# Turning one tile of widened reciprocal roots instead of eight tiles of scaled x, with x also loaded as columns

## What is computed

```python
def rms_norm(x, g):
    y = x * lax.rsqrt(jnp.mean(x * x, axis=-1, keepdims=True) + RMS_EPS)
    return y * g
u = rms_norm(h, pre_norm[l])                      # 4096 x 1024
proj = jnp.einsum('bsd,de->bse', u, w_in[l])      # 4096 x 3072
```

## Time and profile before

| | |
|---|---|
| device time, median of 3 | 2173.83 us |
| profiled execution: its time, its span | 2177.77 us, 2175.6 us |
| PE busy | 2055.3 us (94%) |
| DVE busy | 1561.1 us (72%) |
| ACT busy | 1350.1 us (62%) |
| POOL busy | 115.2 us (5%) |
| moved by DMA | 401.40 MB, mean 184 GB/s |

### The profile page before, as it was taken

The page is one execution under the profiler, slowest core; times in us unless marked ns, Lnnn a source line. Parts: engine busy times, 40 slices in busy tenths (PEclk is TensorE's granted clock), DMA queues, the critical chain, the costliest instruction groups (busy, mean ns, idle before and its releaser), DMA issues. The chain is left out here.

```text
span 2175.6 us, 39344 instructions
## 1 busy us (share of the span) xinstructions
PE 2055.3 (94%) x12892; PEld 1717.4 (79%) x12892; DVE 1561.1 (72%) x4410; ACT 1350.1 (62%) x3520; POOL 115.2 (5%) x116
## 2 busy tenths in 40 slices
PE   5999799999999999998889999999899998899998
PEld 4787678888888888886777888888778887688886
DVE  6575574546655574445589899799799997888887
ACT  6453454544555464343699999899689997533333
POOL 1232210000000000001200000000000000000000
PEclk7999999999999999999899999899999999999999
DMA  4466666768577757578976686596869895355543
GB/s 156 151 218 221 179 227 174 227 206 249 159 224 233 201 191 243 197 246 259 219 146 129 128 173 135 115 179 120 164 147 214 228 267 168 103 164 174 171 158 114
DMA packets 351736, 401.40 MB, mean 184 GB/s; under 512 B 105616, under 2 KB 255248, under 8 KB 346688
## 3 DMA queue, kind: packets, MB, share of 16 engines
q1 hardware_dynamic: 343120, 364.80, 61.2%
q0 software_dynamic: 8432, 34.30, 5.2%
HBM read 255.62 MB, written 143.39 MB: 183 GB/s over the span
## 5 line engine op out<-in xcount | busy, mean ns | idle before, releaser
L854 PE MATMUL p_ps<-p_u_hi,p_w_hi 128*128 128x512 f32 x1344 | 537.3, 400 | 36.3 <-DVE p_p_c L739 17.1
L856 PE MATMUL p_ps<-p_u_hi,p_w_lo 128*128 128x512 f32 x1344 | 528.7, 393 | 0.0
L855 PE MATMUL p_ps<-p_u_lo,p_w_hi 128*128 128x512 f32 x1344 | 528.4, 393 | 0.0
L570 DVE TENSOR_TENSOR p_w_lo<-p_w_raw,p_w_hi 128x512 fp32r<-128x512 f32 x336 | 250.6, 747 | 340.2 <-ACT p_w_hi L423 338.5
L1621 ACT ACTIVATE probs<-probs,a_stat 128x256 f32<-128x256 f32 (+1 forms) x896 | 433.4, 489 | 50.3 <-DVE a_stat L1455 47.1
L423 ACT ACTIVATE p_w_hi<-p_w_raw 128x512 fp32r<-128x512 f32 x336 | 210.7, 628 | 339.1 <-PE p_ps L856 297.9
L854 PEld LDWEIGHTS p_ps<-p_u_hi,p_w_hi 128*128 128x128 f32 x1344 | 255.7, 190 | 96.3 <-issue 17.8
L856 PEld LDWEIGHTS p_ps<-p_u_hi,p_w_lo 128*128 128x128 f32 x1344 | 255.4, 190 | 55.0
L855 PEld LDWEIGHTS p_ps<-p_u_lo,p_w_hi 128*128 128x128 f32 x1344 | 256.0, 190 | 51.3
L1455 DVE CUSTOM_DVE_ANT_0 probs<-a_ps_s,fixed 128x256 f32<-128x256 f32 (+1 forms) x704 | 251.2, 396 | 56.4 <-PE a_ps_s L1354 53.1
L1408 PE MATMUL a_ps_o<-a_pT,a_v 128*64 128x128 f32 x3320 | 256.3, 285 | 23.6 <-ACT a_pT L1645 21.9
(11 more groups left out here) (202 smaller groups left out, 2752.5 us busy)
## 6 DMA issues: line engine op xcount, KB each, us to landing
p_w_raw<-in_w_in SPq DMA_DIRECT2D x156, 256.0 KB, 3.5
p_w_raw<-scratch_w_s SPq DMA_DIRECT2D x144, 256.0 KB, 3.6
scratch_qk_hi<-p_out_a SPq DMA_DIRECT2D x80, 256.0 KB, 4.0
scratch_qk_lo<-p_out_b SPq DMA_DIRECT2D x80, 256.0 KB, 3.9
a_v<-scratch_v SPq DMA_DIRECT2D x40, 512.0 KB, 7.7
scratch_gate<-p_out_a SPq DMA_DIRECT2D x64, 256.0 KB, 3.9
scratch_v<-p_out_a SPq DMA_DIRECT2D x256, 64.0 KB, 2.3
a_gate<-scratch_gate SPq DMA_DIRECT2D x64, 256.0 KB, 6.1
```

What stands on the lines that cost most here:

```text
L570: nc.vector.tensor_tensor(w_lo[:, m % 3, :, :], w_raw[:, entry(j, g), :, :], w_hi[:, m % 3, :, :].bitcast(F32), ALU.subtract).then_inc(w_l ...
L854: nc.tensor.matmul(bank, hi, u_hi[j][:, k, :], start=j < 2 and k == 0, stop=False, skip_group_check=True)
L855: nc.tensor.matmul(bank, hi, u_lo[j][:, k, :], start=False, stop=False, skip_group_check=True)
L856: last = nc.tensor.matmul(bank, lo, u_hi[j][:, k, :], start=False, stop=k == KH - 1, skip_group_check=True)
```

## The change

x is given to the kernel a second time, transposed (`x_columns`, 1024 x 4096). It is loaded straight to the place in `raw` where the turned rows were put. The rows of x are still loaded, for the squares alone. ACT's `scale` goes away. DVE spreads the 128 reciprocal roots of a tile, one per partition, over 128 columns (`widen`); PE turns this one block, so that every partition holds the roots of the 128 tokens along its row; and DVE multiplies the eight blocks of columns by them and by the gain of the channel, in place, with eight instructions instead of one.

```diff
+        spread = sb("spread", [P, P])
-        def front_bank(t):
-            place = (0, 1, 2, 0, 2, 0, 2, 0)[t]
+        def front_place(t):
+            place = (0, 1, 3, 5, 6, 0, 1, 5)[t]
+            return (ps_t[:, place, 0:P] if place < 2 else ps[:, place - 2, 0:P])
...
                 def load_x_first(t):
                     if t >= 4:
-                        sp.wait_ge(u_turned, t - 3)
+                        sp.wait_ge(squared, t - 3)
...
+                def load_columns(c, done):
+                    sp.dma_start(raw[:, c, :, :], io["x_columns"].rearrange("(k p) n -> p k n", p=P)[
+                        :, :, c * CHUNK:(c + 1) * CHUNK]).then_inc(done, 16)
...
+                load_x_first(2)
+                load_x_first(3)
+                load_columns(0, m_stored)
                 for j in (0, 3, 4, 6):
                     load_w(j, 0)
-                load_x_first(2)
-                load_x_first(3)
-                for t in range(4, XT):
-                    load_x_first(t)
+                load_x_first(4)
+                load_x_first(5)
+                sp.wait_ge(consts, 48)
+                load_columns(1, consts)
+                load_x_first(6)
+                load_x_first(7)
...
-                def scale(n, src):
-                    act.wait_ge(inverted, n + 1)
-                    nc.scalar.activation(src, src, ACT.Copy, scale=ss[:, n % 2, 3:4]).then_inc(scaled, 1)
...
+                def widen(n):
+                    dve.wait_ge(inverted, n + 1)
+                    if n:
+                        dve.wait_ge(u_turned, n)
+                    nc.vector.tensor_copy(spread[:], ss[:, n % 2, 3:4].broadcast_to([P, P])).then_inc(scaled, 1)
+
-                def keep(n, src):
+                def keep(n, roots):
                     dve.wait_ge(u_turned, n + 1)
...
-                    nc.vector.tensor_tensor(raw[:, t // 4, :, (t % 4) * P:(t % 4 + 1) * P], src.rearrange("p a (k n) -> p (a k) n", n=P),
-                                            gain[:].unsqueeze(2).broadcast_to([P, KD, P]), ALU.mult).then_inc(raw_ready, 1)
+                    if quarter and t == 0:
+                        dve.wait_ge(ahead.w_loaded, 32 * quarter)
+                    for k in range(KD):
+                        place = raw[:, t // 4, k, (t % 4) * P:(t % 4 + 1) * P]
+                        last = nc.vector.scalar_tensor_tensor(out=place, in0=roots, scalar=gain[:, k:k + 1], in1=place,
+                                                              op0=ALU.mult, op1=ALU.mult)
+                    last.then_inc(raw_ready, 1)
...
+                def turn_roots(n, dst):
+                    pe.wait_ge(scaled, n + 1)
+                    nc.tensor.transpose(dst, spread[:], ident[:]).then_inc(u_turned, 1)
...
+                def load_columns(quarter):
+                    pool.wait_ge(u_lo_ready, NJ * quarter)
+                    for c in range(2):
+                        at = quarter * QT + c * CHUNK
+                        pool.dma_start(raw[:, c, :, :], io["x_columns"].rearrange("(k p) n -> p k n", p=P)[
+                            :, :, at:at + CHUNK]).then_inc(ahead.w_loaded, 16)
...
-                        pool.wait_ge(u_turned, n)
+                        pool.wait_ge(squared, n)
...
+                    if i == 0 and g >= NP:
+                        load_columns(quarter + 1)
```

More of the change, by code:

```diff
@@ L405, in _ @@
                     slot(G, j)
-                sp.wait_ge(m_stored, 48)
+                sp.wait_ge(m_stored, 64)
                 for b in range(3):
@@ L432, in high_u @@
                     elif j == 6:
[L433 removed]
+                        act.wait_ge(squared, XT)
                     nc.scalar.activation(u_hi[j][:], u_raw[j], ACT.Copy).then_inc(u_hi_ready, 1)
@@ L483, in _ @@
                     root(t)
-                    scale(t, x_first[:, t % 4, :])
                     if t in (1, 2):
@@ L531, in slot @@
                             root(n)
-                        if j == 2:
-                            scale(n, x_next)
                     if quarter == 3 and i == 1:
@@ L584, in add_u @@
                         dve.wait_ge(raw_ready, XT * (quarter + 1))
-                        dve.wait_ge(u_turned, XT * (quarter + 1))
+                        dve.wait_ge(squared, XT * (quarter + 1))
                     else:
@@ L600, in invert @@
                     nc.vector.reciprocal(ss[:, b, 3:4], ss[:, b, 2:3]).then_inc(inverted, 1)
-                def keep(n, src):
+                def widen(n):
[4 more added lines that the diff above has]
+                def keep(n, roots):
                     dve.wait_ge(u_turned, n + 1)
+                    quarter, t = divmod(n, XT)
                     if n == 0:
                         dve.wait_ge(consts, 48)
-                    t = n % XT
-                    nc.vector.tensor_tensor(raw[:, t // 4, :, (t % 4) * P:(t % 4 + 1) * P], src.rearrange("p a (k n) -> p (a k) n", n=P),
-                                            gain[:].unsqueeze(2).broadcast_to([P, KD, P]), ALU.mult).then_inc(raw_ready, 1)
+                        dve.wait_ge(m_stored, 16)
+                    if n == 4:
+                        dve.wait_ge(consts, 64)
+                    if quarter and t == 0:
[5 more added lines that the diff above has]
+                    last.then_inc(raw_ready, 1)
                 def low(g, block):
@@ L706, in _ @@
                     invert(t)
+                    widen(t)
                     if t:
-                        keep(t - 1, front_bank(t - 1))
+                        keep(t - 1, front_place(t - 1))
                     if t in (2, 3):
@@ L712, in _ @@
                         low_u(0, FIRST[t - 6])
-                keep(XT - 1, front_bank(XT - 1))
+                keep(XT - 1, front_place(XT - 1))
                 add_u(0, "T1")
@@ L746, in differ @@
                     if n == 0:
-                        dve.wait_ge(ahead.w_loaded, 16 * KD)
-                        dve.wait_ge(m_stored, 48)
+                        dve.wait_ge(ahead.w_loaded, 96 + 16 * KD)
+                        dve.wait_ge(m_stored, 64)
                     else:
@@ L783, in slot @@
                             invert(n)
+                            widen(n)
                         if j == 4:
-                            keep(n, ps_t[:])
+                            keep(n, ps_t[:, 0, 0:P])
                     if quarter < 3 and i == NP - 2 and j in (1, 4):
@@ L827, in turn @@
                     last.then_inc(done, 1)
+                def turn_roots(n, dst):
+                    pe.wait_ge(scaled, n + 1)
+                    nc.tensor.transpose(dst, spread[:], ident[:]).then_inc(u_turned, 1)
                 for t in range(XT):
-                    pe.wait_ge(scaled, t + 1)
-                    if t >= 3:
-                        pe.wait_ge(raw_ready, (1, 3, 4, 5, 6)[t - 3])
-                    turn(t, x_first[:, t % 4, :], front_bank(t), u_turned)
+                    if t >= 5:
+                        pe.wait_ge(raw_ready, (1, 2, 4)[t - 5])
+                    turn_roots(t, front_place(t))
                 def product(g, j):
@@ L897, in slot @@
                         n = (quarter + 1) * XT + t
-                        pe.wait_ge(scaled, n + 1)
                         pe.wait_ge(raw_ready, n)
                         wait_v(g)
-                        turn(n, x_next, ps_t, u_turned)
+                        turn_roots(n, ps_t[:, 0, 0:P])
                     if quarter == 3 and i in (2, 3) and j == 3:
@@ L954, in _ @@
                     nc.gpsimd.tensor_tensor(s4, a12, s2, ALU.subtract).then_inc(w_added, 1)
+                    if g == 1:
+                        load_columns(1)
                 pool.wait_ge(multiplied, NJ * (3 * NP + 4) + 7)
@@ L1908, in _ @@
                 rounds(act, scalar_round, lambda g: g.scalar_parts(act))
-                act.wait_ge(ahead.w_loaded, 16 * KD + 48)
+                act.wait_ge(ahead.w_loaded, 96 + 16 * KD + 48)
                 act.wait_ge(groups[1].values_done, groups[1].TOTAL)
```

7 lines of the change are left out of this document (3 added, 4 removed).

## The result

| | before | changed |
|---|---|---|
| device time, median | 2175.01 us (2167.49 to 2193.32, 18 runs) | 2185.14 us (2175.91 to 2196.52, 18 runs) |
| profiled execution: time, span | 2177.77, 2175.6 us | 2180.97, 2179.2 us |
| PE, DVE, ACT busy | 2055.3, 1561.1, 1350.1 us | 2030.6, 1594.9, 1317.0 us |
| moved by DMA | 401.40 MB | 418.17 MB |

The ratio of changed to before is 1.0046, 95% interval 1.003 to 1.0063. The forecast was 2165 us, the range 2156 to 2180: the result lies outside it and on the other side of no change. In the second batch of runs (experiment 1) the same kernel came to 1.0057. PE's busy time fell by 24.7 us, and the kernel is about 10 us slower.

What follows compares the result with a forecast made beforehand. PE was taken to bound projection quarters 1 to 3, the making of first operands its start. Terms: -18.5 steady tiles, +2 first quarter, +1.5 joins, +6 front, +0.5 late rows = -8.5 us, giving a 2165 us median, range 2156 to 2180.

Steps and rivals of the forecast that it cites:

- three places to cost: The 24 steady tiles, the front with its 8 tiles, and the new loads.
- Quarter 1's have 5 us more: Columns of quarters 2 and 3 are needed only at 370.38 us; those of quarter 1 have 5 us more.
- The term I had for the first quarter: Eight of 24 turns (6.2 us) lie where PE sometimes waits for weights; 2 us given back, bounds 0 and 6.2.
- Steady tiles: PE in 24 tiles: seven of eight transposes go, 0.77 us a tile, 18.5 us gained, bounds 10.6 and 21.
- the joins: DVE's longer `keep` delays the second `join`: 0.5 us for one tile a quarter, 1.5 us lost, bounds 0 and 6.
- DVE's duration: `keep` as eight pieces of 128 columns takes 2.1 us, 0.9 more than now, bounds 1.1 and 2.7.
- overlap down to 1.1: Rival, more gain: DVE's eight pieces overlap to 1.1 us and loads don't hold the front; 2159 us, chance 0.18.
- The front: Start of the projection: late rows and four longer keeps start T1 at 41.7 instead of 35.74; 6 us lost.
- Rows behind the columns: Rows queued behind 4.2 MB of columns on POOL's queue land 3 us early; 0.5 us lost, bounds 0 and 18.
- The rival that carried my chance for slower: Rows behind the columns land 6.6 us late and cost 9 us, for quarters 2 and 3; 2183 us, chance 0.12.

Runs made afterwards that it cites:

- experiment 1: The changed kernel run again, unedited, for a second trace; 2186.88 us, ratio 1.0057 to the kernel before.
- experiment 3: The kernel before plus POOL's 4.2 MB load of quarter 1's columns, used for nothing; 2178.90 us, ratio 1.0018 to the kernel before.
- experiment 7: The changed kernel with only one of eight channel groups of quarter 1's columns loaded (0.5 MB); 2180.70 us, ratio 1.0014 to the kernel before.
- experiment 5: The changed kernel with the front (tiles 0 to 7) made the old way, burst kept; 2182.17 us, ratio 1.0034 to the kernel before.
- experiment 12: The changed kernel with the old front and an eighth of quarter 1's columns loaded; 2170.85 us, ratio 0.9977 to the kernel before.
- experiment 8: The changed kernel with `keep` as one instruction, without the gain; 2180.57 us, ratio 1.0024 to the kernel before.
- experiment 9: Only tiles 16 to 31 new, and `keep` one slot later in groups 8 and 9; 2162.49 us, ratio 0.9938 to the kernel before.
- experiment 2: The changed kernel with tiles 0 to 15 made the old way, only 16 to 31 new; 2165.11 us, ratio 0.9967 to the kernel before.
- experiment 4: The changed kernel with tiles 8 to 15 made the old way, so new front and no burst; 2178.53 us, ratio 1.0022 to the kernel before.
- experiment 6: The changed kernel with the second 2.1 MB columns load of a quarter issued three groups later; 2186.72 us, ratio 1.0058 to the kernel before.
- experiment 11: The changed kernel with the front's two columns loads cut to an eighth, POOL filling in ones; 2184.07 us, ratio 1.0035 to the kernel before.
- experiment 10: Only tiles 16 to 31 made the new way, run again unedited; 2164.82 us, ratio 0.9958 to the kernel before.

## Why the prediction was wrong

**The step that failed: the first quarter and its loads.** The prediction named three places to cost, and priced the burst of columns by one victim alone, the rows behind it on POOL's own queue, for quarters 2 and 3; of quarter 1 it said only "Quarter 1's have 5 us more", which is about when the columns themselves are needed. It never asked what 4.2 MB do in the first quarter to the queue beside it, although it had the earlier trace rows on the table, PE waiting for the chain of weights, and the earlier trace rows, weights that take 8.2 us to land under a like burst. There PE's timeline had no wait, and from that I concluded too much: in the first quarter the loads and stores of the sums are in the chain that PE waits for, and SP stands until the stores have landed (8.2 us instead of 0.6); in the later quarters the sums are only loaded, not made and stored. With the burst alone PE waits 7.59 us (experiment 3), with an eighth of it 0.88 (experiment 7). Priced by ratios: 7 to 9 us (experiment 7 against the changed kernel), 12 with the old front (experiment 5 against 12), 4 in the old kernel (experiment 3); each of these is uncertain by 5 to 7 us. The term I had for the first quarter was +2, bounds 0 and 6.2, and nothing for the burst there; it should have been about +8 for the burst, and the whole 6.2 for the eight turns that gain nothing.

**Steady tiles: right on PE, half eaten by DVE.** 0.77 us a tile was forecast and 0.76 is what the turn gave (0.79 less 0.03). But a quarter gained 3.7 us where 6.2 less 0.5 was expected. The term that was mis-sized is the joins: one tile a quarter was thought to be late by 0.5 us, and it is two, by 0.75 and 0.71 (in group 8 L623 runs from 499.11 for 2.15 us, the join behind it starts only at 501.18). I had done the arithmetic for group 2, where it is just in time, and waved at the slots with the rotary part. Experiments 8 and 9 show it from two sides: with the short keep or the later slot these waits are gone and the quarter takes 235.1 or 235.3 us.

**DVE's duration: right.** 2.1 us forecast for the eight pieces, 2.15 measured (340 ns each, as worked out from the earlier trace rows); no overlap down to 1.1.

**The front: right.** 6 us forecast, 6.75 in T1 and in the first copy. Both halves of the mechanism are there, late rows (5.46 us of waiting ahead of the square of tile 6) and four keeps behind them. It seems to go on into the quarter undiminished: experiments 12 and 7 differ in the front alone, and their marks are 7.0 us apart, in one trace each. By the ratios of experiments 2 and 4 the front costs 12 us, uncertain by 6.

**Rows behind the columns: right, nothing.** In quarter 1 the first square of the next tiles starts without a wait for its rows, at 364.22, although rows behind a burst were seen to take 17.4 us; in quarter 2, at 601.54, it is the same. The rival that carried my chance for slower fell, and the one that came was not on the list.

**The sum again, with what was measured.** The marks, by what the first quarter has (experiments 6, 8 and 11, which change a part in another way, are left out):

| kernel | front | burst | tiles 8 to 15 | mark, us |
|---|---|---|---|---|
| before, experiments 2, 9, 10 | old | none | old | 352.06, 341.79, 341.28, 346.45 |
| experiment 3 | old | whole | old | 350.94 |
| experiment 4 | new | none | old | 354.58 |
| experiment 12 | old | an eighth | new | 347.61 |
| experiment 5 | old | whole | new | 356.99 |
| experiment 7 | new | an eighth | new | 354.62 |
| changed, experiment 1 | new | whole | new | 362.46, 363.59 |

The first row has a mean of 345.4 and the last one of 363.0: the first quarter ends 17.6 us later. Step by step, in single traces, it is 6 to 9 us for the front, 5.5 to 9.4 for the burst and 0 to 6 for the new tiles. Less 7.4 us for quarters 1 and 2 at 3.7 each, the sum is +10.2 us. The ratios say +10 and +12. The forecast had -8.5: +6 for the front, -3.7 for the first quarter with its burst and its tiles, where about +10 came, -11.3 for quarters 1 and 2, where -7.4 came, and +0.5 for late rows, where nothing came.

What stays open is the size of each part. Marks with the same first quarter lie up to 10.8 us apart from one execution to the next, and each ratio between two experiments is uncertain by 6 us or so. That the whole burst costs more than an eighth of it is seen in the waits of SP and PE in every trace; its price can't be brought closer than these ranges. That SP's wait for the stores is the link is read from the code and from SP's waits, in kernels with and without the burst; no run takes this wait away and leaves the burst.

## What to carry to other kernels

A bulk load must be priced by every queue that moves bytes at that time, and first of all by the chain that the bounding engine is already seen waiting for, not only by what stands behind it on its own queue. A saving in the steady part is worth nothing where the engine waits anyway: make such a change only from the stretch on where it pays (experiment 9), and leave the start alone. And when an instruction on a helper engine grows by a microsecond, check every slot where it stands ahead of a hand-over, since one slot later may be free.

## What was not expected of the hardware

PE's long waits cost more than their length. In the changed kernel the granted clock from 120 to 140 us, with the wait of 6.54 us, was 0.83; in experiment 7, with 0.88 us at that place, it was 1.00:

```profile
120.00:140.00 20.00, 13.46 (x51) 10.55 (x50) 11.92 (x21) 7.86 (x14) 6.42 (x5) 0.83 0.66 201
```

```profile
120.00:140.00 20.00, 18.74 (x81) 14.63 (x80) 17.50 (x35) 10.62 (x18) 7.45 (x7) 1.00 0.65 214
```

The matmul that ends the wait of 6.54 us takes 0.79 us at the lower of the two levels (1.2 GHz), the one after 0.88 us takes 0.50. From 127.8 to 132 us the granted clock was 0.50, and ten matmuls start in that time where 18 would at 0.23 us each: an estimate of 2 us on top of the wait. Short waits can do the same where two stand close together: behind those of 2.46 and 2.17 us in experiment 12 the next matmul takes 0.77 us.

One 128x128 transpose between two products is nearly free, 0.03 us, where eight took 0.79. And the stages behind the projection, which no experiment touches, varied by 8 us between executions: from the wait for a join at about 1014 us to the end of the span it was 1161.6 us before, 1162.7 in the changed kernel and 1170.0 when that was run again. From the turn of V in group 1 of quarter 3 to the end, where all 14 profiled kernels run the same instructions, it was 1341.5 to 1355.2 us. That is more than the whole effect of the change, so two profiled executions can't be subtracted from each other.
